# Gathering the tokens of two experts at once as rounded products, one wide product for the last queries' sums, and gate tiles copied out earlier

## The reference

```python
def moe_swiglu(x, router, wg, wu, wd):
    logits = (x @ router).astype(jnp.float32)
    top_val, top_idx = lax.top_k(logits, TOP_K)
    top_w = jax.nn.softmax(top_val, axis=-1)
    gates = jnp.sum(jax.nn.one_hot(top_idx, N_EXPERTS, dtype=jnp.float32) * top_w[..., None], axis=-2)
    y = jnp.zeros_like(x)
    for e in range(N_EXPERTS):
        y = y + gates[..., e:e + 1].astype(x.dtype) * swiglu(x, wg[e], wu[e], wd[e])
    return y
```

## Time and profile before

| | us |
|---|---|
| three timed runs, median | 2033.01 |
| lowest, highest | 2032.62, 2035.44 |
| the profiled execution | 2034.68 |
| its span in the trace | 2032.9 |

### The profile page before, as it was taken

One profiled execution on the slowest core, in us unless ns is written; L12 is line 12 of the kernel. 1 busy time (PEld: TensorE's weight loads), 2 busy tenths in 40 slices (PEclk: granted clock), 3 DMA queues, 4 the chain that ended last, 5 costly groups with the idle time before them and its releaser, 6 DMA issues.

```text
span 2032.9 us, 36044 instructions
## 1 busy us (share of the span) xinstructions
PE 2001.4 (98%) x15296; PEld 1761.3 (87%) x15296; DVE 1496.4 (74%) x1311; ACT 1199.0 (59%) x1076; POOL 53.6 (3%) x36
## 2 busy tenths in 40 slices
PE   8999999999999999999999999999999999999998
PEld 6978999999998888899988888888888888888886
DVE  6656356765455766438578898888889889898896
ACT  5454453543343545445467777777777777777675
POOL 0003100000000001200000000000000000000000
PEclk9999999999999999999999999999999999999999
DMA  7432035444442322105459899898998989899895
GB/s 239 172 111 97 4 133 201 166 166 172 187 162 106 142 106 86 41 27 225 179 224 380 344 358 373 323 372 336 369 367 335 373 334 364 349 359 372 326 376 199
DMA packets 75038, 485.60 MB, mean 239 GB/s; under 512 B 13480, under 2 KB 14632, under 8 KB 17192
## 3 DMA queue, kind: packets, MB, share of 16 engines
q1 hardware_dynamic: 73816, 481.93, 61.3%
q10 hardware_dynamic: 1104, 1.92, 0.3%
HBM read 482.08 MB, written 1.74 MB: 238 GB/s over the span
## 4 chain that ended last, share of the span: by engine, by line
PE 92%; DVE 4%; ACT 2%; DMA 1%; issue 1%; POOL 0%; ACTq 0%; SPq 0%; DVEq 0%
PE PS L576 26%; PE PS L578 25%; PE PS L577 25%; PE PS L956 6%; DVE area L1910 1%; PE PS L1282 1%; PE PS L1291 1%; DVE WL L1910 1%; ACT WH L1442 1%; PE PS L914 1%; DMA ring<-in_weights 1%; PE PS L731 1%; DVE YEL L2515 0%; PE PS L1358 0%; PE PS L847 0%
## 5 line engine op out<-in xcount | busy, mean ns | idle before, releaser
L1910 DVE TENSOR_TENSOR WL<-ring,WH 128x2048 fp32r<-128x2048 f32 x410 | 934.4, 2290 | 218.0 <-ACT WH L1442 109.3
L1442 ACT ACTIVATE WH<-ring 128x2048 fp32r<-128x2048 f32 x336 | 643.1, 1916 | 158.5 <-PE PS L578 149.0
L576 PE MATMUL PS<-WH,XGH 128*128 128x512 f32 x896 | 353.7, 395 | 0.2 <-DVE XGL L1910 0.2
L578 PE MATMUL PS<-WL,XGH 128*128 128x512 f32 x896 | 349.7, 390 | 0.0
L577 PE MATMUL PS<-WH,XGL 128*128 128x512 f32 x896 | 349.1, 390 | 0.0
L578 PE MATMUL PS<-XL,WH 128*128 128x272 f32 (+1 forms) x704 | 202.5, 288 | 0.0
L1434 ACT ACTIVATE WH<-ring 128x2048 fp32r<-128x2048 f32 x74 | 141.3, 1910 | 102.0 <-PE PS L578 102.0
L578 PEld LDWEIGHTS PS<-WL,XGH 128*128 128x128 f32 x896 | 168.1, 188 | 35.8
L576 PEld LDWEIGHTS PS<-WH,XGH 128*128 128x128 f32 x896 | 168.3, 188 | 34.6 <-DVE WL L1910 0.5
L577 PEld LDWEIGHTS PS<-WH,XGL 128*128 128x128 f32 x896 | 168.4, 188 | 33.5
L576 PE MATMUL PS<-WH,HTH 128*128 128x512 f32 x448 | 176.7, 394 | 0.6
(11 more groups left out here) (350 smaller groups left out, 3432.7 us busy)
## 6 DMA issues: line engine op xcount, KB each, us to landing
ring<-in_experts SPq DMA_DIRECT2D x336, 1024.0 KB, 6.6
ring<-in_weights SPq DMA_DIRECT2D x114, 1024.0 KB, 6.9
ring<-in_weights SPq DMA_DIRECT2D x4, 576.0 KB, 4.4
ring<-in_weights SPq DMA_DIRECT2D x4, 512.0 KB, 4.0
cst<-in_consts SPq DMA_DIRECT2D x1, 1731.0 KB, 7.4
hT<-in_stream ACTq DMA_DIRECT2D x2, 544.0 KB, 7.0
out<-area SPq DMA_DIRECT2D x4, 256.0 KB, 2.0
bias_line<-lin SPq DMA_DIRECT2D x1, 672.0 KB
```

The costliest lines, as they stand in the source:

```text
L576: pe.matmul(o, lh, rh, start=first, stop=False, skip_group_check=True)
L578: return pe.matmul(o, lh, rl, start=False, stop=last, skip_group_check=True)
L1442: act.activation(WH[(BASE + j + 1) % 3][:, :], ring[b][:, 2048 * (j % 2):2048 * (j % 2) + 2048], ACT.Copy).then_inc(S("w_hi"), 1)
L1910: tt = lambda o, a_, b_, op: dve.tensor_tensor(o, a_, b_, op)
```

## The change

1. **Gather.** The normed rows are kept split, TOKH (made by ACT in place of `hnT`) and TOKL (made by DVE, `token_low`). Two experts are gathered together: PICK holds both selection matrices side by side, 256 columns, and a gather is four rounds of 8 rounded products (`gather_round`): round 0 the high parts of blocks 0 to 3, round 1 their low parts, rounds 2 and 3 the same for blocks 4 to 7. The result of a high round is copied to XGH by ACT, that of a low round to XGL by DVE. All rounds of a pair use banks 2 and 3, except those ahead of the first expert, which have banks of their own.
2. **Places.** The expert loop runs over pairs: 3 rounds with the bodies of two experts, and the last pair written out. An even expert gathers nothing. An odd one runs round 0 behind the first half of u6, round 1 behind its second half, round 2 behind the first half of d5 and the turn, round 3 behind the second half of d5. Ahead of the first expert `gate_weights`, which sets `route_flag`, stands behind the low parts on DVE.
3. **Sums.** The four products of 16 columns become two of 32, whose right side reads the 16 columns twice.
4. **Gate tiles.** The tiles that are finished by the steps ahead of the turn (`early`) are copied out, and their weight tile split, ahead of ACT's wait for the turn. With (5, 3) in layer 0 `early` never exceeds the count before, so that nothing moves there; in layer 1 it moves one tile in each of units 1, 2 and 3.

```diff
@@ -201,7 +201,9 @@
 
         WH = [pinned(f"WH{i}", [P, 2048], at1 + 4 * 2048 * 2 * i) for i in range(3)]
         WL = [pinned(f"WL{i}", [P, 2048], at1 + 4 * 2048 * (2 * i + 1)) for i in range(3)]
-        XGH, XGL = [pinned(nm, [P, D], at2 + 4 * o) for nm, o in (("XGH", 8448), ("XGL", 9472))]
+        XGH, XGL = pinned("XGH", [P, 2, D], at_xn), pinned("XGL", [P, 2, D], at2 + 4 * 8448)
+        TOKH, TOKL = pinned("TOKH", [P, 2, D], at_xh), pinned("TOKL", [P, 2, D], at2 + 4 * KT * T)
+        PICK = pinned("PICK", [P, 2, 2, SLOTS], at_slots)
...
+        FIRST_BANKS = 0, 2, 6, 4
...
@@ -460,18 +471,23 @@
...
-            with eng.Fori(0, NE - 1) as e:
-                body(eng, e, e, 0, False)
-            body(eng, NE - 1, NE - 1, 0, True)
+            PAIRS = NE // 2
+            with eng.Fori(0, PAIRS - 1) as i:
+                body(eng, i * 2, i * 2, 0, False, 0, i)
+                body(eng, i * 2 + 1, i * 2 + 1, 0, False, 1, i)
+            body(eng, NE - 2, NE - 2, 0, False, 0, PAIRS - 1)
+            body(eng, NE - 1, NE - 1, 0, True, 1, PAIRS - 1)
...
@@ -915,8 +931,8 @@
                     for g in range(2):
                         pe.matmul(PS[:, b + g, P:T], C("negones"), spA[:, g, T:416], start=False, stop=False, skip_group_check=True)
                     for g in range(2):
-                        for o in (2 * P, 400):
-                            ins = pe.matmul(PS[:, b + g, o:o + 16], C("negones"), spA[:, g, 416:432], start=False, stop=True, skip_group_check=True)
+                        last_queries = PS[:, b + g, P:416].rearrange("p (a n) -> p a n", n=144)[:, :, P:144]
+                        ins = pe.matmul(last_queries, C("negones"), bc(spA[:, g, 416:432], [P, 2, 16], 1), start=False, stop=True, skip_group_check=True)
                     ins.then_inc(S("arg_done"), 1)
...
@@ -1274,16 +1290,24 @@
             unread(3)
...
-            def gather(wait_for, mid=None):
-
-                pe.wait_ge(S("e_sel"), wait_for)
-                for k in range(KT):
+            def gather_round(r, bank):
+                token = (TOKH, TOKL)[r % 2]
+                for i in range(4):
+                    k = 4 * (r // 2) + i
                     for t in range(2):
-                        ins = pe.matmul(PS[:, 2 + k // 4, (k % 4) * SLOTS:(k % 4 + 1) * SLOTS], hnT[:, t, k * P:(k + 1) * P],
-                                        SEL[:, t, :], start=(t == 0), stop=(t == 1))
-                    if mid and k == 3:
-                        ins.then_inc(S(mid), 1)
+                        ins = round_product(PS[:, bank + i // 2, (i % 2) * 2 * SLOTS:(i % 2 + 1) * 2 * SLOTS], token[:, t, k * P:(k + 1) * P],
+                                            PICK[:, t, :, :].rearrange("p x s -> p (x s)"), t == 0, t == 1)
                 ins.then_inc(S("e_xg"), 1)
+
+            def gather_pair(p, r):
+
+                if r == 0:
+                    pe.wait_ge(S("e_sel"), p + 1)
+                elif r % 2:
+                    pe.wait_ge(S("e_xgh"), p * 2 + (r // 2 + 1))
+                else:
+                    pe.wait_ge(S("e_xgl"), p * 2 + 1)
+                gather_round(r, 2)
...
                         turn_hidden(n, f - 1)
+                    if odd and not last and kind == "u" and f == FG - 1:
+                        gather_pair(p + 1, half)
                     if (kind, f, half) == ("u", 3, 1):
...
                     if (kind, f, half) == ("d", FG - 2, 0):
                         turn_hidden(n, FG - 1)
-                        if not last:
-                            gather(n + 2)
+                    if odd and not last and (kind, f) == ("d", FG - 2):
+                        gather_pair(p + 1, 2 + half)
                 if not last:
-                    pe.wait_ge(S("e_xgl"), n + 2)
-                    half_products(n + 1, 0)
+                    if odd:
+                        pe.wait_ge(S("e_xgl"), p * 2 + 4)
+                    half_products(n + 1, 0, 1 - odd)
                     pe.wait_ge(S("e_stc"), n * 2 + (2 - run))
                     scatter()
...
                 if isinstance(run, int) and run == 0:
 
-                    gather(1, "router_pe")
+                    pe.wait_ge(S("e_sel"), 1)
+                    gather_round(0, FIRST_BANKS[0])
+                    pe.wait_ge(S("router_dve"), ROUTER["first_low"])
+                    gather_round(1, FIRST_BANKS[1])
+                    gather_round(2, FIRST_BANKS[2])
                     pe.wait_ge(S("router_dve"), ROUTER["rows_low"])
+                    gather_round(3, FIRST_BANKS[3])
+                    pe.wait_ge(S("e_xgh"), 1)
+                    pe.wait_ge(S("e_xgl"), 1)
...
@@ -1631,6 +1667,8 @@
                     if u == 0:
                         act.wait_ge(S("ya_copied"), at("ya_copied", l, 3))
                         act.activation(YH[0][:, :, :], yA[:, :, :], ACT.Copy).then_inc(S("x_hi"), 1)
+                    early = (KT + sum(GATE_STEPS[l]) * u + GATE_STEPS[l][0]) // KT
+                    gates_out(gates_after(l, u - 1), early)
...
                     if u + 1 < N_UNITS[l]:
                         weighted_keys(u + 1)
-                    gates_out(gates_after(l, u - 1), gates_after(l, u))
+                    gates_out(early, gates_after(l, u))
...
             act.wait_ge(S("router_dve"), ROUTER["rstd"])
-            for t in range(2):
-                for q in range(2):
-                    ins = act.activation(hnT[:, t, 512 * q:512 * q + 512], PS[:, 2 + t + 2 * q, :], ACT.Copy, scale=MR[:, 184 + t:185 + t])
+            for q in range(2):
+                for t in range(2):
+                    ins = act.activation(TOKH[:, t, 512 * q:512 * q + 512], PS[:, 2 + t + 2 * q, :], ACT.Copy, scale=MR[:, 184 + t:185 + t])
...
+            def gathered_high(p, r, bank):
+                act.wait_ge(S("e_xg"), p * 4 + (r + 1))
+                act.activation(gathered_view(XGH, r), gathered_banks(bank), ACT.Copy).then_inc(S("e_xgh"), 1)
...
+                if odd and not last:
+                    at_half(events, "u", FG - 1, 0, 2).append((lambda r: gathered_high(p + 1, r, 2), 0))
+                    at_half(events, "d", FG - 2, 0, 2).append((lambda r: gathered_high(p + 1, r, 2), 2))
...
-                gathered_high(act, n + 2)
...
                 def select_tokens(f):
-                    if last:
+                    if last or not odd:
                         link_e(2, dve.memset(small[:, 51:52], 0.0))
                         return
-                    link_e(2, dve.tensor_copy(MR[:, 162:164], slots[:, :, bass.ds(e + 1, 1)]))
-                    dve.wait_ge(S("e_xg"), n + 1)
+                    link_e(2, dve.tensor_copy(next_slots, slots[:, :, bass.ds(e + 1, 2)]))
+                    dve.wait_ge(S("e_xg"), p * 4 + 4)
                     select_next(S("e_sel"))
...
+                if odd and not last:
+                    at_half(events, "u", FG - 1, 1, 2).append((lambda r: gathered_low(p + 1, r, 2), 1))
+                    at_half(events, "d", FG - 2, 1, 2).append((lambda r: gathered_low(p + 1, r, 2), 3))
...
+            def gathered_low(p, r, bank):
+                dve.wait_ge(S("e_xg"), p * 4 + (r + 1))
+                dve.tensor_copy(gathered_view(XGL, r), gathered_banks(bank)).then_inc(S("e_xgl"), 1)
...
             def select_next(sem):
                 for t in range(2):
-                    ins = dve.tensor_scalar(SEL[:, t, :], C("iota", 0, SLOTS), MR[:, 162 + t:163 + t], None, ALU.is_equal)
+                    for x in range(2):
+                        ins = dve.tensor_scalar(PICK[:, t, x, :], C("iota", 0, SLOTS), MR[:, 166 + 2 * t + x:167 + 2 * t + x], None, ALU.is_equal)
                 ins.then_inc(sem, 1)
+
+            def token_low(q):
+
+                for t in range(2):
+                    cols = slice(512 * q, 512 * q + 512)
+                    ins = dve.scalar_tensor_tensor(TOKL[:, t, cols], PS[:, 2 + t + 2 * q, :], MR[:, 184 + t:185 + t], TOKH[:, t, cols].bitcast(F32),
+                                                   ALU.mult, ALU.subtract)
+                ins.then_inc(S("router_dve"), 1)
...
                 select_next(S("e_sel"))
                 first = isinstance(run, int) and run == 0
                 if first:
+                    dve.tensor_reduce(small[:, 41:42], PS[:, 6, 16:24], AX.X, ALU.max)
+                    dve.wait_ge(S("router_act"), ROUTER["rows"])
+                    token_low(0)
+                    token_low(1)
+                    gathered_low(0, 1, FIRST_BANKS[1])
+                    gathered_low(0, 3, FIRST_BANKS[3])
                     gate_weights()
-                    dve.wait_ge(S("router_act"), ROUTER["rows_high"])
-                    tt(XGL[:, 0:512], PS[:, 2, :], XGH[:, 0:512].bitcast(F32), ALU.subtract).then_inc(S("router_dve"), 1)
-                    dve.wait_ge(S("e_xgh"), 1)
-                    tt(XGL[:, 512:D], PS[:, 3, :], XGH[:, 512:D].bitcast(F32), ALU.subtract).then_inc(S("e_xgl"), 1)
```

(4 more changed lines are left out.)

62 lines of the change are left out of this document (29 added, 33 removed).

## The result

| | median us | runs from to | profiled span | mean granted clock |
|---|---|---|---|---|
| before, beside it | 2034.22 | 2032.62 to 2037.43 | 2032.9 | 0.996 |
| changed | 2047.67 | 2046.64 to 2050.09 | 2045.2 | 0.990 |

The ratio is 1.0063 (95% interval 1.0048 to 1.0078): slower by 13 us, where 15 us less had been forecast. The forecast was wrong, its sign and its range too.

What follows compares the result with a forecast made beforehand. TensorE, busy 98% of the span, was taken to bound the kernel. 11.6 us for the gather, 3.2 for the sums and 4.5 for the gate tiles, less 4 for the loop, made 15.3: 2033.0 to 2017.7 us, range 2011 to 2026.

Steps and rivals of the forecast that it cites:

- Gather: Expert gathers in paired rounds of products at 0.12 us: 11.6 us less after waits and the costs ahead of the first expert.
- Flag: Behind the first half of expert 0: TensorE stands 0.3 us for the flag, then 0.4 for the register read (0 to 1.5).
- rival of two passes: Gather's round products of 256 columns run as two passes, 0.45 us each, 57 us instead of 15.4: 2059 us; chance 0.03.
- Sums: Last queries' sums: half the records go, 8 calls at 0.40 us, 3.2 us less (2.5 to 3.8).
- gate tiles: Layer 1's branch C: both TensorE stops for POOL go and the clock stays up, 4.5 us less (2 to 5).
- Loop: TensorE's doubled expert loop body: 2 us lost at each of two taken branches, 4 us in all (0 to 4.7 each).
- long fetch: Rival at the loop's branches: stops of 4.7 us plus 1.5 at the lower clock, 12.4 instead of 4, 2026.1 us; chance 0.11.
- branch free: Rival at the loop's branches: the longer body is held or fetched in time, no cost, 2013.7 us; chance 0.30.
- Gate tiles bring little: Rival in layer 1's branch C: the stop moves elsewhere, 2 us or less instead of 4.5, 2020.5 us; chance 0.10.
- Loads as the limit: Rival in the expert loop: even experts leave 3.6 us less for the ring to fill, some us lost, 2022 us; chance 0.08.
- signs that it named for being wrong: Round products above 0.12 us, TensorE waiting for `w_lo` near odd experts' ends, or the gate tiles' stops staying.
- its signs for the branch: Instruction packets inside the expert loop, and a TensorE gap right behind the scatter ahead of experts 2 and 4.

Runs made afterwards that it cites:

- b_pe_pair_loop: Kernel before with only TensorE's expert loop run over pairs of experts, the other engines' loops kept; 2051.58 us, ratio 1.0076.
- a_xgh_high: Changed kernel with XGH at the start of area2 (178688), loop over pairs kept; 2030.64 us, ratio 0.9972.
- b_xgh_256: Kernel before with XGH moved down 256 bytes to 212224, a multiple of 256 and not of 512; 124.14 us a scatter, one run.
- b_xgh_low_aligned: Kernel before with XGH in low memory at 59392, a multiple of 1024; ratio 0.9998, 124.14 us a scatter.
- a_written_out: Changed kernel with the three rounds of its loop over pairs written out on every engine, XGH's address kept; 2032.83 us, ratio 0.9983.
- b_gates: Kernel before with the gate tiles' edit alone; 2032.67 us, ratio 0.9981.
- a_both_mended: Changed kernel with XGH at the start of area2 and the loop over pairs written out on every engine; 2019.66 us, ratio 0.9917.
- a_tensor_written_out: The last kernel run: changed kernel with XGH at 59136 and the loop over pairs written out for TensorE alone; 2018.64 us, ratio 0.9919.

## Why the prediction was wrong

**Gather: right.** Forecast 11.6 us less in all. An expert without a gather behind it takes 120.6 (120.64 and 120.87 in the last kernel) against 124.14: 3.5 less. One with the four rounds takes 124.8: 0.65 more, for 3.84 - 3.57 + 0.3 = 0.57 worked out. Three of each make 8.6; expert 0 is 2.3 shorter too, its missing gather less the stop at the flag.

**Flag: too small by half.** 1.48 us (1.25 in the last kernel) for 0.7, inside its bounds.

**One figure of the rival of two passes was off.** With the rest as forecast the change turns to a loss once a round product is above 0.24 us (15.4 and 15.3 over 128), not 0.27. They took 0.12, so nothing hung on it.

**Sums and gate tiles: right.** By the distances 3.6 for 3.2, and 4.9 for 4.5.

**Loop: the term that was mis-sized.** The forecast took 2 us for each of two taken branches, between 0 and 4.7. Measured were 7.6 and 6.8, in b_pe_pair_loop 7.9. The step that failed was the price of a stop: a transfer of 2.0 to 6.6 us, "less the scatter's 1.9 which is issued ahead of the branch". The scatter hid nothing: the instruction packet begins 1.7 to 2.5 us after the scatter is over, takes 1.0, less than any transfer that the forecast had looked at, and then 1.8 pass before a product starts. So most of the 5.28 and 4.43 is not the transfer but what stands ahead of it and behind it, which had no term. And the 2 us and more of a half-speed clock were left to a rival. That rival (long fetch, 12.4 us for the two) had the stop and the clock behind it and nearly the size, 14.4, though not what the stop is made of. The Trainium skill (Runtime: NRT & Kernel Launch, Instruction fetch mechanics) says of a taken branch whose target isn't in the current two-page window that it forces a fetch of the target's page before execution goes on, and gives this as a reason why kernels prefer unrolling. The trace agrees for the body of 1132 products, with stops of 5.28 and 4.43 us, a packet in each, and none once it is written out. It doesn't bear out the window of two pages of 256 instructions: the body of before, 566 products and as many weight loads, is longer than that and shows neither stop nor packet. The prediction cited this rule as making the loss certain and still gave "branch free" a chance of 0.30: the rule should have weighed more.

**XGH's address: missing altogether.** The change has a new line of `pinned` for XGH, and the prediction has no term for it, nor a rival. It asked of each moved instruction what it costs and never of a moved operand. No row of before could show it, since there XGH and XGL both stood on multiples of 256; the address can be worked out from the allocation alone, though, and the question could have been a rival. It cost 14 us.

**The router's clock: not clearly from the change.** With the upper clock throughout the router the first half would have begun at about 1022 (a_xgh_high: 1022.21), 10 us earlier than before and not 5. From the first call of layer 0's sums to the first half, which leaves out a fall of the clock at 83 us that some profiles have, the kernel before takes 899.9 us, a_xgh_high 889.6 and the changed kernel 896.1. Of the 10.3 less in a_xgh_high 1.7 at most is a fall at 715 that it lacks; the rest stands against 7 forecast. The changed kernel loses 6.5 of it again in the router. But b_xgh_256, which differs from the kernel before in an address alone, first written at the router's end, also ran its router at the lower level (0.72 from 1012 to 1022 us, first half at 1037.44, where b_xgh_low_aligned has 1.00 and 1030.76), while a_xgh_high, whose instructions there are those of the changed kernel, did not. So one stream of instructions meets both levels. It seems to change from run to run of one kernel: the ten runs of a_xgh_high have mean clocks from 0.989 to 0.997, though only one of them has a trace. All four runs of the changed kernel had a mean clock of 0.990 or 0.991, of which the two stops make 0.003 (a_written_out, without them, had 0.993) and the router most of the rest. If a low mean clock stands for a slow router, the kernel before met it in 27 of its 76 runs beside the experiments (0.994 or less) and the changed kernel with its variants in 24 of 42 (0.994 or less, 0.992 where the two stops are in). That hints that the change makes it more frequent; it does not show it, since b_gates, which leaves the router and the experts alone, has 6 of 11.

**The other rivals.** Two passes per round product: no, a round of eight takes 1.12. Gate tiles bring little: no. Loads as the limit: not in the changed kernel, where TensorE never waits for WL in the loop. In a_both_mended expert 2 took 122.14 us for 120.5, with a wait of 0.6 for WL in the stretch. The trace has the loads behind it: in that expert ACT waits six times for the ring, 8.4 us in all, DVE then waits for ACT and TensorE for DVE, where in expert 4 ACT waits once for 1.0. The same comes in expert 1 of a_xgh_high (125.61 for 124.8; ACT waits 11.0 us for the ring). In the last kernel it is gone. So that rival is real in single turns, and worth about 1 us each time.

**Together.** Against the kernel before: -10.6 (experts' gathers and flag), -5.1 (all ahead of the first half, the router's clock in it), +14.4 (branches), +14.1 (address) are +12.8; the spans differ by +12.3. Against the forecast span of 2017.6 the measured one is 27.6 us longer: 10.4 from the branches (14.4 for 4), 14.1 from the address, and 3 from the rest: 6.5 lost to the router's clock, less what the falls at 83 and 715 us, which its profile lacks, and the stretches that gained more than forecast give back. The rival "branch free" stood at 2013.7 us, 19.3 less than before. a_tensor_written_out, with the two causes taken away, is 16.4 less by the medians (2018.64 against 2035.05), where two of its four runs have a low mean clock; that its profiled execution took 2013.42 is in part luck, as it is the fastest of the four. Part by part, by the distances above, what the prediction had priced came out near its price, and the loss is one term of the wrong size and one that was not there. None of the signs that it named for being wrong came; of its signs for the branch both did, the packets in the loop and the gap behind the scatter.

## What to carry to other kernels

Place weight buffers that TensorE loads thousands of times on multiples of 256 bytes, and print the addresses whenever a change moves one: no wait in a profile names this, only a mean duration that is 5 ns longer than that of the same product with aligned weights. Ask of every loop body that grows whether it still stays loaded (instruction packets inside the loop tell that it doesn't), and price each taken branch at the stop plus the slow clock behind it. A bound for a step should not be cut by cover that nobody has seen work.

## What the runs showed that was not expected

- **Alignment of weights.** With 128 columns of 4 bytes, a weight row is 512 bytes. At 128 past a multiple of 256 a 512-column product takes on average 8 ns more for each load of that buffer (1.8 us / 224), at 192 past it 4 ns (0.86 / 224, one profile), at 0 nothing, at low and high addresses alike. Other remainders were not tried. The records of XGH's loads stay at 188 ns; with XGL moved, the load behind XGL's rises from 188 to 192. What in the engine does it is not shown.
- **Taken branch.** 4.4 to 5.4 us of stop and 2 to 3 lost behind it, most of it at half speed, with a TensorE body of 1132 products (eight branches in four profiles); none with 566. The instruction packet takes 1.0 of it. Lengths between the two were not tried.
- **Clock without a stop.** The clock fell to 1.2 GHz with TensorE busy throughout, in the router, products of 8 columns among them, in some profiles and not in others that have the same instructions there. Twenty runs of the kernel before beside a_xgh_high went from 2031.6 to 2035.1 us where the mean clock was 0.997, and from 2040.4 to 2041.9 where it was 0.992. So a difference of 4 us between two single profiles of this kernel is read from distances inside them, not from their spans.
